# Two softmax attentions inside one kernel: turns placed ahead of the slabs' quarters, values' and outputs' low parts in other slots, quarters dealt with pauses

## Chip, cores and metric

The kernel runs on one core of one Trainium2 chip, as one launch. The metric is the time of the device in microseconds; the engines are PE (TensorE, matmuls and transposes), DVE (VectorE), ACT (ScalarE), POOL (GpSimd, which here issues the weight DMAs and negates weights) and SP (issues a few DMAs).

## What is computed

The reference is two transformer blocks, 512 tokens by 1024 channels, in float32. The change lies in two of its attentions, both over 16 heads of 64 channels:

```python
# first block: dilated windows; one mask and one bias by distance for all three groups
s = q @ k.T - slope * dist          # 512 x 512 per head, causal
p = exp(s - max); o = (p @ v) / sum(p)
x = x + (g_a * y_a + (g_b * (o @ w_attn_out))) @ w_out     # g = sigmoid(x @ w_gate)
# second block: attention over chosen keys
p = softmax(where(chosen, q @ k.T / 8, -inf)); o = p @ v
y = (o * silu(x @ w_g)) @ w_out_a
```

The kernel computes the first block's three dilated groups as one softmax over all keys with a bias for how many groups hold a key. Every matmul is three: each float32 operand is split into a high part (rounded for TensorE) and a low part, and high x high, low x high and high x low are added in PSUM.

## The kernel before

A stream of 231 weight slabs (128 x 1024 values, 512 KB) runs through four slots; POOL issues the two DMAs of each. A slab is 24 matmuls of 512 columns for one output tile of 128 channels. Between large projections stand the attentions, here called the first (`a`, over the phase "gates", 12 slabs) and the second (`b`, over the phase "g2", 8 slabs). Each attention walks over `PAIRS` = 8 pairs of heads. The order on each engine is the order in which the code is written, in three functions: `softmax_attention` for PE and one `attention` each for ACT and DVE. Semaphores tie them.

For pair i and query block q (0 to 3, the causal width is q+1 blocks):

- `scores(i, q)` on PE writes both heads' scores into one of two sets of banks (parity of q); `biased(i, q)` on DVE adds the bias or mask, takes the row extreme and stores to `PROBS`; `prob(i, q, h)` on ACT takes the exponential.
- `turn_p(i, q)` on PE transposes the probabilities into two "turn" banks; `pt_hi` (ACT) and `pt_lo` (DVE) copy the high and low parts to `PT_HI`, `PT_LO`, and only then is the bank free. `turn_p(i, 2)` needs the banks that `turn_p(i, 0)` and `turn_p(i, 1)` filled, `turn_p(i, 3)` those of `turn_p(i, 2)`, `turn_qk(i+2)` those of `turn_p(i, 3)`.
- `inverse` (DVE) and `spread` (ACT) make the inverse sums; `turn_inverse` (PE) transposes them into the out bank, from which `inverse_t` (ACT, first attention) or `inverse_gate` (DVE, second, times the gate) takes them to `INVERSE`.
- `values(i)` on PE needs `pt_lo(i, 3)`, `v_lo(i)` and `INVERSE`; `output(i)` on DVE takes its result, `out_hi` (ACT) and `out_lo` (DVE) split it.
- `turn_qk(i)`, `qk_hi(i)`, `qk_lo(i)` transpose and split the queries and keys of a pair, into the same two turn banks.

A slab of the weight phase is cut into quarters of 6 matmuls, which `fill(i, q)` deals out in four slots of a pair. `A_FILL` and `B_FILL` say how many quarters each slot gets, a row for each pair and one for the end. All slabs of an attention share one PSUM bank (`SLAB_BANK`), so a slab's first quarter waits until the slab before has been read: by a tanh on ACT (`gate`), in the second attention by a DVE instruction after it that reads the bank too. In the second attention two slabs are done ahead of the loop (`B_EARLY`), the second in the out bank.

Of the kernel before, what the change touches and what calls it, by code (L numbers as in the profile page):

```python
# [97 lines left out]
A_FILL = 5 * [[2, 1, 1, 2]] + 2 * [[1, 1, 1, 1]] + [[1, 1, 0, 0]] + [[4, 4]]  # L98
B_FILL = 6 * [[1, 1, 1, 0]] + [[1, 1, 1, 0]] + [[0, 0, 0, 0]] + [[2, 1]]
# [52 lines left out]
def program(nc, x, wstream, consts, small, lnv, out):  # L152
    with ExitStack() as ctx:
# [257 lines left out]
        def _(pe):  # L411
# [91 lines left out]
            def softmax_attention(a, name, table, early):  # L503
# [83 lines left out]
                for i in range(PAIRS):  # L587
                    scores(i, 0)
                    fill(i, 0)
                    if i:  # L590
                        turn_p(i - 1, 2)
                    scores(i, 1)
                    fill(i, 1)
                    if i:
                        turn_p(i - 1, 3)
                        turn_inverse(i - 1)
                    scores(i, 2)
# [6 lines left out]
                    fill(i, 3)  # L604
                    turn_p(i, 0)
                    turn_p(i, 1)
                turn_p(PAIRS - 1, 2)
# [213 lines left out]
        def _(act):  # L821
# [35 lines left out]
            def attention(a, sq, sk, name, table, early):  # L857
# [73 lines left out]
                for buf in (V_HI, V_LO):  # L931
                    for h in range(2):
                        d = slice((1 - h) * HD, (2 - h) * HD)
                        act.activation(buf[:, :, h, d], zero[:, 0:1].unsqueeze(2).to_broadcast([P, TT, HD]), ACT.Copy)\
                            .then_inc(sem(f"{a}_v_zero"), 1)
                qk_hi(0)
                for i in range(PAIRS):
                    last = i == PAIRS - 1
                    prob(i, 0, 0)
                    prob(i, 0, 1)  # L940
                    if i == 0 and early:
                        gate(0)
                    gates(i, 0)
                    if i:
                        pt_hi(i - 1, 2, 0)
                        pt_hi(i - 1, 2, 1)
                        spread(i - 1)
                    prob(i, 1, 0)
                    prob(i, 1, 1)
                    if i == 0 and early:  # L950
                        gate(1)
                    gates(i, 1)
                    if i:
                        pt_hi(i - 1, 3, 0)
                        pt_hi(i - 1, 3, 1)
                        if a == "a":
                            inverse_t(i - 1)
                    prob(i, 2, 0)
                    prob(i, 2, 1)
                    gates(i, 2)  # L960
                    if not last:
                        qk_hi(i + 1)
                    prob(i, 3, 0)
                    prob(i, 3, 1)
                    gates(i, 3)
                    pt_hi(i, 0)
                    pt_hi(i, 1)
                    v_hi(i)
                    if i:
                        out_hi(i - 1)  # L970
                i = PAIRS - 1
# [240 lines left out]
        def _(dve):  # L1212
# [32 lines left out]
            def attention(a, sq, sk, bias, name, table, early):  # L1245
                t0 = TILE0[name]

                def head_bias(i):
                    for h in range(2):
# [85 lines left out]
                if a == "a":  # L1335
                    head_bias(0)
                qk_lo(0)
                for i in range(PAIRS):
# [7 lines left out]
                    if i == 0 and early:  # L1346
                        gate(0)
                    gates(i, 0)
                    biased(i, 1)
                    if i:  # L1350
# [516 lines left out]
```

## Time and profile before

| | before |
|---|---|
| time, median of 3 runs | 1773.61 us (1773.6 to 1778.68) |
| the profiled execution's own time | 1777.48 us |
| its span, first to last instruction | 1775.4 us |
| mean granted clock of TensorE | 0.968 |
| PE busy | 1647.2 us (93%) |
| weight loads (PEld) | 1344.9 us (76%) |
| DVE, ACT, POOL busy | 928.3, 542.6, 589.6 us |
| first attention, 320.02 to 491.06 us | 171.04 us |
| second attention, 1164.87 to 1335.74 us | 170.87 us |

A "granted clock" of 1 is 2.4 GHz, of 0.5 is 1.2 GHz, and a number between is a stretch with both. Busy times of PE overlap from one matmul to the next, so the step from one start to the next start is what a matmul costs. The two attentions are named by the start of their first `scores` and the end of their last `values`.

### The profile page before, as it was taken

The page shows a single profiled execution, that of the slowest core. Times are in us where ns is not written, and L with a number is a line of the kernel's source. Part 1 is how long each engine was busy: PE and PEld are TensorE (multiplying, and loading weights), DVE is VectorE, ACT ScalarE, POOL GpSimd, SP SyncE. Part 2 cuts the span into 40 slices and gives each one's busy share as a digit, 9 for nine tenths or more (in the row PEclk, how much of TensorE's full clock was granted, in tenths as well). Part 3 has the DMA queues.
Part 4 walks back from the last instruction along what each step waited for, and adds up shares of the span by engine and source line. Part 5 has one row for each costly group of instructions (what it writes and reads, how often), then busy time and mean ns, then how long its engine had stood idle before and what let it go on. Part 6 is the DMA issues. An engine that isn't in the chain of part 4 may idle for free.

```text
span 1775.4 us, 20032 instructions
## 1 busy us (share of the span) xinstructions
PE 1647.2 (93%) x7808; PEld 1344.9 (76%) x7808; DVE 928.3 (52%) x1672; ACT 542.6 (31%) x1079; POOL 589.6 (33%) x698
## 2 busy tenths in 40 slices
PE   6999999999899899999998989978879799999985
PEld 5888878777787788888887768756658678888874
DVE  2999996466451444333001249835641606766654
ACT  3101131556400322222000130145540226667640
POOL 3445434221144344444443424411003232222211
PEclk9999999999999999999999999989989899999988
DMA  8888878443279698888886858832118484545434
GB/s 223 194 189 194 196 156 188 102 85 74 57 169 223 148 194 194 198 191 192 188 189 143 191 105 179 191 81 48 27 34 176 109 178 95 110 97 103 95 93 109
DMA packets 69134, 253.23 MB, mean 143 GB/s; under 512 B 7600, under 2 KB 7728, under 8 KB 68912
## 3 DMA queue, kind: packets, MB, share of 16 engines
q0 software_dynamic: 66528, 242.25, 63.3%
q1 hardware_dynamic: 1968, 7.60, 1.2%
q10 hardware_dynamic: 544, 2.10, 0.3%
q8 instruction: 62, 1.02, 0.2%
q14 instruction: 32, 0.26, 0.1%
HBM read 249.82 MB, written 2.10 MB: 142 GB/s over the span
## 4 chain that ended last, share of the span: by engine, by line
PE 85%; DVE 6%; ACT 5%; issue 2%; DMA 1%; SPq 0%; DVEq 0%; POOL 0%; ACTq 0%
PE PSUM L416 26%; PE PSUM L417 25%; PE PSUM L418 25%; PE PSUM L650 2%; ACT PROBS L878 2%; DVE PT_LO L1295 1%; PE PSUM L531 1%; PE PSUM L426 1%; ACT PT_HI L891 1%; PE PSUM L633 1%; PE PSUM L552 1%; PE PSUM L519 1%; DMA SMALLS<-small 1%; DVE MASK L1614 1%; DMA W_LO<-wstream 1%
## 5 line engine op out<-in xcount | busy, mean ns | idle before, releaser
L404 POOL DMA_DIRECT2D W_HI<-wstream x231 | 128.2, 555 | 1031.8 <-PE PSUM L418 1031.3
L416 PE MATMUL PSUM<-X_HI,W_HI 128*128 128x512 f32 x872 | 355.3, 407 | 29.4 <-DVEq L1312 17.6
L417 PE MATMUL PSUM<-X_LO,W_HI 128*128 128x512 f32 x872 | 345.6, 396 | 0.0
L418 PE MATMUL PSUM<-X_HI,W_LO 128*128 128x512 f32 x872 | 345.4, 396 | 0.0
L394 POOL TENSOR_SCALAR W_LO<-W_HI 128x1024 fp32r<-128x1024 f32 x231 | 253.2, 1096 | 20.4 <-DMA W_HI<-wstream 16.2
L416 PE MATMUL PSUM<-W_HI,X_HI 128*128 128x512 f32 x608 | 238.6, 392 | 9.2 <-DVE X_LO L1217 2.6
L398 POOL DMA_DIRECT2D W_LO<-wstream x231 | 208.3, 902 | 99.8 <-POOL W_LO L394 99.8
L417 PE MATMUL PSUM<-W_LO,X_HI 128*128 128x512 f32 x608 | 237.8, 391 | 0.0
L418 PE MATMUL PSUM<-W_HI,X_LO 128*128 128x512 f32 x608 | 237.8, 391 | 0.0
L416 PEld LDWEIGHTS PSUM<-X_HI,W_HI 128*128 128x128 f32 x872 | 166.7, 191 | 78.9 <-issue 43.7
L418 PEld LDWEIGHTS PSUM<-X_HI,W_LO 128*128 128x128 f32 x872 | 166.8, 191 | 36.6
L417 PEld LDWEIGHTS PSUM<-X_LO,W_HI 128*128 128x128 f32 x872 | 167.2, 192 | 32.4
L1475 DVE SCALAR_TENSOR_TENSOR CONV<-CONV_IN,SMALLS,CONV 128x512 f32<-128x512 f32 x240 | 186.3, 852 | 0.0
L416 PEld LDWEIGHTS PSUM<-W_HI,X_HI 128*128 128x128 f32 x608 | 115.0, 189 | 35.9 <-ACT INDEX_RELU L1107 3.1
L1562 DVE SCALAR_TENSOR_TENSOR GATE_A<-PSUM,SMALLS,GATE_A 128x511 f32<-128x511 f32 x88 | 66.0, 750 | 143.0 <-ACT GATE_A L1071 141.4
L418 PEld LDWEIGHTS PSUM<-W_HI,X_LO 128*128 128x128 f32 x608 | 114.8, 189 | 24.2
L417 PEld LDWEIGHTS PSUM<-W_LO,X_HI 128*128 128x128 f32 x608 | 114.9, 189 | 23.6
L878 ACT ACTIVATE PROBS<-PROBS,soft_stats 128x128 f32<-128x128 f32 (+3 forms) x128 | 70.9, 555 | 133.3 <-DVE soft_stats L1283 133.3
L855 ACT ACTIVATE QKV<-PSUM 128x512 f32<-128x512 f32 x48 | 24.8, 605 | 225.1 <-PE PSUM L418 225.1
L1243 DVE TENSOR_TENSOR GATE_B<-PSUM,GATE_B 128x512 f32<-128x512 f32 x16 | 9.9, 683 | 156.8 <-PE PSUM L418 156.8
L1295 DVE TENSOR_TENSOR PT_LO<-PSUM,PT_HI 128x256 fp32r<-128x256 f32 (+2 forms) x96 | 54.8, 598 | 70.9 <-ACT PT_HI L891 70.1
L1071 ACT ACTIVATE GATE_A<-PSUM,SMALLS 128x512 f32<-128x512 f32 x44 | 34.4, 782 | 165.9 <-PE PSUM L418 165.2
(226 smaller groups left out, 2668.7 us busy)
## 6 DMA issues: line engine op xcount, KB each, us to landing
W_HI<-wstream POOLq DMA_DIRECT2D x231, 512.0 KB, 4.0
W_LO<-wstream POOLq DMA_DIRECT2D x231, 512.0 KB, 5.9
GATE_A<-x SPq DMA_DIRECT2D x4, 512.0 KB, 6.1
GATE_B<-x SPq DMA_DIRECT2D x1, 2048.0 KB, 17.4
NORM_GAINS<-lnv ACTq DMA_DIRECT2D x2, 1024.0 KB, 5.5
out<-GATE_B SPq DMA_DIRECT2D x4, 512.0 KB, 2.8
CONST<-consts SPq DMA_DIRECT2D x1, 1032.0 KB, 10.9
SMALLS<-small SPq DMA_DIRECT2D x1, 245.0 KB, 12.1
```

The source lines that it names most:

```text
L394: pool.tensor_scalar(W_LO[:, r, :], W_HI[:, r, :].bitcast(F32), -1.0, 0.0, ALU.mult, ALU.add)\
L398: pool.dma_start(W_LO[:, r, :], wstream[n], accum_op=ALU.add).then_inc(w_lo_in[r], 16)
L404: pool.dma_start(W_HI[:, n % SLOTS, :], wstream[n]).then_inc(w_hi_in[n % SLOTS], 16)
L416: pe.matmul(o, lh, rh, start=start, stop=False)
L417: pe.matmul(o, lh, rl, start=False, stop=False)
L418: return pe.matmul(o, ll, rh, start=False, stop=stop)
L650: pe.matmul(o, m, part[:, h, w], start=False, stop=False, skip_group_check=True)
L878: act.activation(p, p, ACT.Exp, scale=-1.0, bias=soft_stats[:, 0, q, h:h + 1], accum_out=soft_stats[:, 1, q, h:h + 1]).then_inc(sem(f"{a}_ ...
L1071: act.activation(FFN_CONV[:, 2 * m + v, :], PSUM[:, 2 * m + v, :], ACT.Identity, scale=SMALLS[:, bass.ds(i * 12 + (S_AT["fw"].start + (2 * ...
L1295: dve.tensor_tensor(pt_block(PT_LO, both, q), src, pt_block(PT_HI, both, q).bitcast(F32), ALU.subtract).then_inc(sem(f"{a}_pt_lo"), 1)
L1475: dve.scalar_tensor_tensor(acc, src, w, acc, ALU.mult, ALU.add).then_inc(step, 1)
L1562: ins = dve.scalar_tensor_tensor(FFN_CONV[:, b, d:], PSUM[:, b, 0:SEQ - d], w, FFN_CONV[:, b, d:], ALU.mult, ALU.add)
```

## The change

Nothing is computed differently; the same instructions run in another order (a wait of DVE on its own earlier work is added in `head_bias`). On PE the turns of probabilities (and of the inverse) stand ahead of the slot's quarters where they stood behind. On ACT `pt_hi` is written ahead of `prob`, `v_hi(i-1)` moves from the end of pair i-1 to the second slot of pair i; in the second attention the two early gates go ahead of and behind `qk_hi(0)`. On DVE `v_lo(i-1)` and `out_lo(i-2)` move into pair i. The two tables of quarters are dealt anew, with an empty slot behind the end of most slabs.

```diff
-A_FILL = 5 * [[2, 1, 1, 2]] + 2 * [[1, 1, 1, 1]] + [[1, 1, 0, 0]] + [[4, 4]]
-B_FILL = 6 * [[1, 1, 1, 0]] + [[1, 1, 1, 0]] + [[0, 0, 0, 0]] + [[2, 1]]
+A_FILL = 2 * [[2, 2, 0, 2], [2, 0, 2, 2], [0, 2, 2, 0]] + [[2, 2, 0, 2], [2, 0, 0, 0]] + [[4, 4]]
+B_FILL = [[1, 1, 1, 1], [0, 1, 1, 1], [1, 0, 1, 1], [1, 1, 0, 1], [1, 1, 1, 0], [1, 1, 1, 1], [0, 0, 1, 0], [0, 1, 0, 0]] + [[2, 0]]
...
                     scores(i, 0)
-                    fill(i, 0)
                     if i:
                         turn_p(i - 1, 2)
+                    fill(i, 0)
                     scores(i, 1)
-                    fill(i, 1)
                     if i:
                         turn_p(i - 1, 3)
                         turn_inverse(i - 1)
+                    fill(i, 1)
                     scores(i, 2)
                     fill(i, 2)
...
                     scores(i, 3)
-                    fill(i, 3)
                     turn_p(i, 0)
                     turn_p(i, 1)
+                    fill(i, 3)
...
+                if early:
+                    gate(0)
                 qk_hi(0)
+                if early:
+                    gate(1)
                 for i in range(PAIRS):
                     last = i == PAIRS - 1
-                    prob(i, 0, 0)
-                    prob(i, 0, 1)
-                    if i == 0 and early:
-                        gate(0)
-                    gates(i, 0)
                     if i:
                         pt_hi(i - 1, 2, 0)
                         pt_hi(i - 1, 2, 1)
+                    prob(i, 0, 0)
+                    prob(i, 0, 1)
+                    gates(i, 0)
+                    if i:
+                        v_hi(i - 1)
                         spread(i - 1)
-                    prob(i, 1, 0)
-                    prob(i, 1, 1)
-                    if i == 0 and early:
-                        gate(1)
-                    gates(i, 1)
-                    if i:
                         pt_hi(i - 1, 3, 0)
                         pt_hi(i - 1, 3, 1)
                         if a == "a":
                             inverse_t(i - 1)
+                    prob(i, 1, 0)
+                    prob(i, 1, 1)
+                    gates(i, 1)
                     prob(i, 2, 0)
                     prob(i, 2, 1)
                     gates(i, 2)
                     if not last:
                         qk_hi(i + 1)
+                    pt_hi(i, 0)
+                    pt_hi(i, 1)
                     prob(i, 3, 0)
                     prob(i, 3, 1)
                     gates(i, 3)
-                    pt_hi(i, 0)
-                    pt_hi(i, 1)
-                    v_hi(i)
                     if i:
                         out_hi(i - 1)
+                v_hi(PAIRS - 1)
...
                 def head_bias(i):
+
+                    after(dve, "a_biased", 8 * i)
...
                     biased(i, 1)
                     if i:
+                        v_lo(i - 1)
                         pt_lo(i - 1, 3, 0)
                         pt_lo(i - 1, 3, 1)
-                    if i == 0 and early:
-                        gate(1)
+                        if a == "b":
+                            inverse_gate(i - 1)
                     gates(i, 1)
-                    if i and a == "b":
-                        inverse_gate(i - 1)
                     biased(i, 2)
+                    if i > 1:
+                        out_lo(i - 2)
...
                     gates(i, 3)
-                    v_lo(i)
-                    if i:
-                        out_lo(i - 1)
                     if a == "a" and not last:
                         head_bias(i + 1)
+                v_lo(PAIRS - 1)
+                out_lo(PAIRS - 2)
```

**PE, second attention, second pair (i = 1), around `scores(1, 1)`** (`[waits tile_free]` on a slab's first matmul is the wait for the shared slab bank). Before:

```order
L531 MATMUL PSUM<-QK_HI 128x256 [waits b_biased]
L531 MATMUL PSUM<-QK_HI 128x256
L531 MATMUL PSUM<-QK_LO,QK_HI 128x256 x2
L531 MATMUL PSUM<-QK_HI,QK_LO 128x256 x2
L416 MATMUL PSUM<-X_HI,W_HI 128x512 [waits tile_free,w_lo_in2]
L417 MATMUL PSUM<-X_LO,W_HI 128x512
L418 MATMUL PSUM<-X_HI,W_LO 128x512
L416 MATMUL PSUM<-X_HI,W_HI 128x512
L417 MATMUL PSUM<-X_LO,W_HI 128x512
L418 MATMUL PSUM<-X_HI,W_LO 128x512
L552 MATMUL PSUM<-CONST,PROBS 128x128 [waits b_pt_lo,b_exp]
L552 MATMUL PSUM<-CONST,PROBS 128x128 x3
```

After:

```order
L531 MATMUL PSUM<-QK_LO,QK_HI 128x256 x2
L531 MATMUL PSUM<-QK_HI,QK_LO 128x256 x2
L552 MATMUL PSUM<-CONST,PROBS 128x128 [waits b_pt_lo,b_exp]
L552 MATMUL PSUM<-CONST,PROBS 128x128 x3
L552 MATMUL PSUM<-CONST,PROBS 128x128 [waits b_pt_lo]
L552 MATMUL PSUM<-CONST,PROBS 128x128 x3
L562 MATMUL PSUM<-CONST,INVERSE 128x128 [waits tile_free,b_spread]
L562 MATMUL PSUM<-CONST,INVERSE 128x128 x3
L416 MATMUL PSUM<-X_HI,W_HI 128x512 [waits tile_free,w_lo_in2]
L417 MATMUL PSUM<-X_LO,W_HI 128x512
L418 MATMUL PSUM<-X_HI,W_LO 128x512
L416 MATMUL PSUM<-X_HI,W_HI 128x512
```

Before, the first quarter of a new slab (with `tile_free`) stood directly behind the scores and ahead of the turns of `PROBS`; now the turns of `PROBS` and of `INVERSE` stand ahead of it.

**ACT, second attention, end of pair 1 and start of pair 2** (`PT_HI` 128x2x128 and 128x2x2x128 are `pt_hi(1, 0)` and `pt_hi(1, 1)`, 128x3x128 is `pt_hi(1, 2)`). Before:

```order
L878 ACTIVATE PROBS,soft_stats<-PROBS,soft_stats 128x512 [waits b_biased] x2
L891 ACTIVATE PT_HI<-PSUM 128x2x128 [waits b_pv,b_pturned]
L891 ACTIVATE PT_HI<-PSUM 128x2x2x128 [waits b_pv,b_pturned]
L872 ACTIVATE V_HI<-QKV 128x4x64 [waits b_pv]
L872 ACTIVATE V_HI<-QKV 128x4x64
L908 ACTIVATE O_HI<-QKV 128x4x128 [waits b_o]
L878 ACTIVATE PROBS,soft_stats<-PROBS,soft_stats 128x128 [waits b_biased] x2
L891 ACTIVATE PT_HI<-PSUM 128x3x128 [waits b_pv,b_pturned] x2
L897 ACTIVATE INVERSE<-soft_stats 128x512 [waits b_o,b_inv]
L878 ACTIVATE PROBS,soft_stats<-PROBS,soft_stats 128x256 [waits b_biased] x2
```

After:

```order
L891 ACTIVATE PT_HI<-PSUM 128x2x128 [waits b_pv,b_pturned]
L891 ACTIVATE PT_HI<-PSUM 128x2x2x128 [waits b_pv,b_pturned]
L878 ACTIVATE PROBS,soft_stats<-PROBS,soft_stats 128x512 [waits b_biased] x2
L908 ACTIVATE O_HI<-QKV 128x4x128 [waits b_o]
L891 ACTIVATE PT_HI<-PSUM 128x3x128 [waits b_pv,b_pturned] x2
L878 ACTIVATE PROBS,soft_stats<-PROBS,soft_stats 128x128 [waits b_biased] x2
L924 ACTIVATE GATE_TANH<-PSUM 128x512 [waits b_gated,slab_done]
L872 ACTIVATE V_HI<-QKV 128x4x64 [waits b_pv]
L872 ACTIVATE V_HI<-QKV 128x4x64
L897 ACTIVATE INVERSE<-soft_stats 128x512 [waits b_o,b_inv]
L891 ACTIVATE PT_HI<-PSUM 128x4x128 [waits b_pv,b_pturned] x2
```

`pt_hi` now stands ahead of the exponentials of its slot, and `V_HI` stands between the narrow exponentials and the spread of `INVERSE` instead of ahead of `O_HI`.

**DVE, first attention, first pair (i = 0): `biased(0, 2)`, `qk_lo(1)`, the gate of slab 0 and `biased(0, 3)`** (ISA is `biased`; 128x384 is q = 2, 128x512 is q = 3). Before:

```order
L1283 ISA PROBS,soft_stats<-PSUM,HEAD_BIAS 128x384 [waits a_scores]
L1283 ISA soft_stats 128x1
L1283 ISA PROBS,soft_stats<-PSUM,HEAD_BIAS 128x384
L1283 ISA soft_stats 128x1
L1256 SCALAR_TENSOR_TENSOR QK_LO<-PSUM,qscale,QK_HI 128x512 [waits a_qk_hi]
L1256 SCALAR_TENSOR_TENSOR QK_LO<-PSUM,SMALLS,QK_HI 128x512 [waits a_qk_hi]
L1305 SCALAR_TENSOR_TENSOR GATE_A<-GATE_TANH,GATE_A 128x512 [waits tile_free]
L1283 ISA PROBS,soft_stats<-PSUM,HEAD_BIAS 128x512 [waits a_scores]
```

After:

```order
L1308 SCALAR_TENSOR_TENSOR GATE_A<-GATE_TANH,GATE_A 128x512 [waits tile_free]
L1286 ISA PROBS,soft_stats<-PSUM,HEAD_BIAS 128x384 [waits a_scores]
L1286 ISA soft_stats 128x1
L1286 ISA PROBS,soft_stats<-PSUM,HEAD_BIAS 128x384
L1286 ISA soft_stats 128x1
L1259 SCALAR_TENSOR_TENSOR QK_LO<-PSUM,qscale,QK_HI 128x512 [waits a_qk_hi]
L1259 SCALAR_TENSOR_TENSOR QK_LO<-PSUM,SMALLS,QK_HI 128x512 [waits a_qk_hi]
L1286 ISA PROBS,soft_stats<-PSUM,HEAD_BIAS 128x512 [waits a_scores]
```

The gate of slab 0, which needs the whole slab, now stands ahead of `biased(0, 2)` and so ahead of `qk_lo(1)`; before it stood behind both.

## Rows read from the trace of the kernel before

**Rows 1.** Busy time by stage: the second attention, then the first; columns as its head.

```profile
core 0: us, PE busy (x) PEld busy (x) DVE busy (x) ACT busy (x) POOL busy (x), PEclk, DMA share, GB/s
1164.87:1335.74 170.87, 137.47 (x777) 107.82 (x778) 90.55 (x244) 82.95 (x230) 15.86 (x19) 0.88 0.21 42
320.02:491.06 171.04, 157.44 (x921) 127.14 (x922) 93.88 (x250) 91.11 (x242) 30.16 (x36) 0.97 0.36 75
```

**Rows 2.** Waits of PE in the second attention: total, times, longest.

```profile
PE PSUM L416 <- DVEq L1312: 17.6, 5, 5.1
PE PSUM L552 <- DVE PT_LO L1295: 11.7, 13, 2.4
```

**Rows 3.** Timelines of ACT, DVE, PE: start us, us, instruction, [idle before <-releaser].

```profile
1185.59 0.57 ACT L924 ACTIVATE GATE_TANH<-PSUM 128x512 f32<-128x512 f32 x1
...
1187.51 0.68 DVE L1309 SCALAR_TENSOR_TENSOR GATE_A<-GATE_TANH,PSUM 128x512 f32<-128x512 f32 x1
...
1188.39 0.76 PE L416 MATMUL PSUM<-X_HI,W_HI 128*128 128x512 f32 x1 [4.56 <-DVEq L1312]
```

**Rows 4.** Windows after two long waits of PE, columns as in rows 1.

```profile
1188.00:1193.00 5.00, 4.61 (x16) 3.96 (x16) 1.16 (x6) 1.69 (x5) 0.00 (x0) 0.50 0.22 43
...
1292.00:1296.00 4.00, 4.00 (x28) 3.65 (x27) 1.61 (x4) 2.16 (x6) 0.00 (x0) 1.00 0.06 11
```

**Rows 5.** Waits of PE in the first attention.

```profile
PE PSUM L552 <- DVE PT_LO L1295: 8.6, 6, 2.4
PE PSUM L416 <- ACT GATE_B L915: 2.6, 3, 1.2
```

**Rows 6.** Timeline of PE at full clock, second attention, 1239 to 1257 us.

```profile
1239.48 0.87 PE L552 MATMUL PSUM<-CONST,PROBS 128*128 128x128 f32 x6
1240.29 0.33 PE L531 MATMUL PSUM<-QK_HI 64*128 64x128 f32 x2
...
1240.77 0.50 PE L416 MATMUL PSUM<-X_HI,W_HI 128*128 128x512 f32 x1
...
1246.89 1.06 PE L552 MATMUL PSUM<-CONST,PROBS 128*128 128x128 f32 x8 [0.83 <-DVE PT_LO L1295]
1247.79 0.60 PE L562 MATMUL PSUM<-CONST,INVERSE 128*128 128x128 f32 x4
...
1249.04 0.50 PE L416 MATMUL PSUM<-X_HI,W_HI 128*128 128x512 f32 x1
...
1250.53 1.04 PE L519 MATMUL PSUM<-CONST,QKV 128*128 128x128 f32 x8
1251.33 0.47 PE L416 MATMUL PSUM<-PT_HI,V_HI 128*128 128x512 f32 x1
...
1256.19 0.87 PE L552 MATMUL PSUM<-CONST,PROBS 128*128 128x128 f32 x6
```

**Rows 7.** Timeline of ACT at the same place.

```profile
1240.32 0.72 ACT L878 ACTIVATE PROBS<-PROBS,soft_stats 128x512 f32<-128x512 f32 x1 [2.64 <-DVE soft_stats L1283]
...
1242.49 0.71 ACT L872 ACTIVATE V_HI<-QKV 128x256 fp32r<-128x256 f32 x2
...
1244.90 0.40 ACT L878 ACTIVATE PROBS<-PROBS,soft_stats 128x128 f32<-128x128 f32 x1 [1.17 <-DVE soft_stats L1283]
...
1245.69 0.84 ACT L891 ACTIVATE PT_HI<-PSUM 128x384 fp32r<-128x384 f32 x2
1246.43 0.62 ACT L897 ACTIVATE INVERSE<-soft_stats 128x512 f32<-128x512 f32 x1
```

**Rows 8.** Timeline of DVE at the same place.

```profile
1242.15 1.17 DVE L1295 TENSOR_TENSOR PT_LO<-PSUM,PT_HI 128x256 fp32r<-128x256 f32 x2 [0.65 <-ACT PT_HI L891]
1243.24 0.75 DVE L1266 TENSOR_TENSOR V_LO<-QKV,V_HI 128x256 fp32r<-128x256 f32 x2
```

**Rows 9.** Chain of waits, first attention, pair 0: start us, us, what.

```profile
330.45 0.58 ACT QK_HI L865
331.05 1.41 DVE QK_LO L1256 x2
```

More of the change, by code:

```diff
@@ L1336, in attention @@
                     head_bias(0)
+                if early:
+                    gate(0)
                 qk_lo(0)
+                if early:
+                    gate(1)
                 for i in range(PAIRS):
@@ L1345, in attention @@
                         pt_lo(i - 1, 2, 1)
-                    if i == 0 and early:
-                        gate(0)
                     gates(i, 0)
@@ L1350, in attention @@
                     if i:
+                        v_lo(i - 1)
                         pt_lo(i - 1, 3, 0)
                         pt_lo(i - 1, 3, 1)
-                    if i == 0 and early:
-                        gate(1)
+                        if a == "b":
+                            inverse_gate(i - 1)
                     gates(i, 1)
-                    if i and a == "b":
-                        inverse_gate(i - 1)
                     biased(i, 2)
+                    if i > 1:
+                        out_lo(i - 2)
                     if not last:
```

## Prediction

> **What bounds the kernel now.** I read the busy time by stage first. Both attentions take 171 us. In the first PE is busy 157.4 of 171.0 us at a granted clock of 0.97; in the second 137.5 of 170.9 us at 0.88 [rows 1]. DVE and ACT are busy 83 to 94 us in each, about half. So no engine but PE is near its limit, and what can be won are PE's waits and the half clock (1.2 GHz) that follows some of them. The rest of the kernel is untouched and comes into the sum at nothing: the weights that the attentions use are far ahead (POOL has 15.9 us of work in 171), and the phases around them keep their order.
>
> Next the waits of PE. In the second attention two groups make 29.3 of its 33.4 idle us: 17.6 us in 5 waits on the gate's DVE instruction, the longest 5.1 us, and 11.7 us in 13 waits of the turns of `PROBS` on `PT_LO` [rows 2]. In the first, 8.6 us are turns on `PT_LO`, 2.6 us are waits on the gate's tanh [rows 5]; its gate releases the bank from ACT alone, so this wait is short there.
>
> Last the single rows. The 4.56 us wait at 1188.39 shows the chain of a bank's release: ACT's tanh starts at 1185.59, the DVE instruction only at 1187.51 behind other work, and PE's quarter follows 0.2 us after its end [rows 3]. The quarter then runs at half clock: the window behind it has a granted clock of 0.50 [rows 4].
>
> **What a pair costs PE.** From start to start at full clock [rows 6]: `turn_p(0)` and `(1)` 0.81 (1239.48 to 1240.29), `scores(0)` 0.48, `turn_p(2)` again six transposes, 0.81, `scores(1)` 0.55 (between `scores(0)` and the next one), `turn_p(3)` 0.90, `turn_inverse` and `scores(2)` 1.25, `turn_qk` 0.80, `values` and `scores(3)` 4.86: 10.46 us. A quarter is 1.49. The second attention is 8 x 10.46, less 0.8 for the first `turn_qk` that lies ahead of it, plus 24 quarters: 82.9 + 35.8 = 118.7 us. Its stretch is 170.9, so 52.2 us are lost: 33.4 idle [rows 1], and some 19 by half clock and by stops inside groups.
>
> **The new order, walked once.** Let T be the end of `scores(i, 3)`; in the rows T is 1239.5.
> ACT: before, the wide exponentials began at T+0.8 and `pt_hi` stood behind them; DVE was free at T+2.0 but waited 0.65 us for it and began `pt_lo(i, 0)` at T+2.7 [rows 7, 8]. Now `pt_hi(i, 0)` and `(i, 1)` run until T+1.5, so `pt_lo` begins at T+2.0 and, at 1.17 us for the two [rows 8], ends at T+3.1. The exponentials (0.72 each) then end at T+2.9, `out_hi` at T+3.5, `pt_hi(i, 2)` (0.74 from start to start) at T+4.3, the narrow exponentials (0.79) at T+5.1, `v_hi` (0.71) at T+5.8, `spread` (0.62) at T+6.4 [rows 7].
> PE, with a quarter in both slots: 0.81 + 1.49 + 0.48 brings `turn_p(i, 2)` to T+2.8; its first half needs `pt_lo(i, 0)` (T+2.4), its second `pt_lo(i, 1)` (T+3.1): no wait. Then 0.81 + 1.49 + 0.55 + 0.90 bring `turn_inverse` to T+6.5, against `spread` at T+6.4: no wait, but no slack either. `values` comes at about T+11, long after `pt_lo(i, 3)` (T+8.3), `v_lo` and `inverse_gate` (T+8.9). So `v_lo` (0.75 [rows 8]) and `out_lo` cost nothing where they now stand; DVE covers them in PE's `values`, and `biased(i+1, 0)` comes over 1 us earlier.
>
> **An empty slot** behind `scores(i, 3)` leaves PE at `turn_p(i, 2)` until T+3.5 in any case: 1.5 us of waiting in the quarter's place. One behind `turn_p(i, 2)` is the same, 1.5 us, at `turn_inverse`. A gate on ACT in the chain adds 0.57 [rows 3]. Empty slots behind `turn_inverse` and `scores(2)` cost nothing. In return no quarter meets an unread bank: the shortest pause is two turns and two scores plus a chain that is over by then. The bank waits, 17.6 us, go.
>
> **Second attention, stalls that I count.** Pair 0: 0.4 on `qk_lo(1)`. Turns of pair 0 with slot (1, 0) empty: 1.5. Gate at (2, 0): 0.55. Slot (4, 3): 1.5. (6, 0), behind a gate: 2.0. (6, 3) and (7, 0): 3.0. End: `turn_p(7, 2)` 1.95, `values(7)` behind the last gate, `pt_lo` and `inverse_gate` 1.85. Sum 12.8, say 13 us. Half clock: the 18.8 us that are lost beside the idle time, over some ten waits of 1.9 us or more in this stretch, are 1.9 us for each; most of these waits go, and I keep 5 us, for the start and two of the waits in the last pairs. 118.7 + 13 + 5 = 136.7 us against 170.9: **34.2 us** less.
>
> **First attention, by differences.** Gone: 2.6 us of bank waits [rows 5] and 0.3 us of a smaller one, about 1 us because more quarters come in twos without a new start, and 2 us of half clock in the last pair, whose waits shrink. The turns' waits: today all of PE's idle time is 13.6 us [rows 1]. New: pair 0 waits 2.5 us, since the gate of slab 0 now stands ahead of `biased(0, 2)`, and `qk_hi` 0.58 a piece and `qk_lo` 1.41 [rows 9] come after it, with nothing between `scores(0, 3)` and the turns that need their bank. Slots (2, 0) and (5, 0) are empty with a gate and `head_bias` on DVE ahead of `pt_lo(i, 2)`: 2.5 us each. (2, 3) and (5, 3): 1.5 each. Gates at (1, 0), (4, 0), (7, 0): 0.4 each. Pair 7: 0.95 and 1.95. Sum 14.7, so 1.1 more than today. Net: 2 + 1 - 1.1, **1.8 us** less.
>
> **Sum.** 36 us off the profiled execution's 1777.5 gives 1741.5. The median of the runs lies 3.9 below it, so 1773.6 - 36 = 1737.6, rounded 1738. Changes under 0.3% (5 us) can't be told from none.
>
> **A rule that speaks against it.** The window behind the 4.56 us wait was at 0.50, but the one behind a 2.64 us wait at 1290, with transposes and `values` in it, stayed at 1.00 [rows 4]; so what decides is not the wait's length alone. The Trainium skill (TensorE: Matmul & The Clock Gate, Part 4: PE-mode transpose) says that transposes do not count as busy for the clock gate as matmuls do. The second of these windows does not show it. What it would do is the second rival.
>
> **Rivals.**
> - *The clock stays low.* Turns now stand together (fourteen to eighteen transposes with scores, no quarter between) beside waits of 1.5 to 2.5 us, at 12 places: 7 in the second attention, 5 in the first. At about 2 us of half clock each, 24 us, against some 7 counted, the time is 17 us higher, 1755. For it: the half clock after waits in [rows 4]; against: the second window there. By the rule of the Trainium skill named above this is the number.
> - *Everything fits.* The empty slots cost only half of what I walked, because engines start a little ahead of my sums, and no half clock is left: 13 + 5 us less 6 and 5, 1727, and down to 1722 if the first attention's three 2.5 us waits fall too.
> - *The waits only move.* The slabs' quarters no longer wait for a bank, but the turns, now ahead of them, wait for `PT_LO` as long: 17.6 us of one kind become 17 of another. Then 1773. Against: the chain of `pt_hi` and `pt_lo` is shortened by 0.7 us in each pair, and the bank waits hung on DVE's late gate, not on it.
> - *Slower: `spread` is late.* `turn_inverse` has no slack against the chain exponentials, gate, `v_hi`, `spread`. PE passes it 14 times. The change loses from where the chain is 36/14 = 2.6 us longer per pair than walked; at 3.2 us it is 1782. ACT would have to take half again as long as its rows say (6.4 us); it is busy only 83 us of 171 [rows 1].
>
> **Chances and range.** Forecast, 1730 to 1746: 0.63. Low clock, 1746 to 1765: 0.17. Everything fits, under 1730: 0.13. Waits only move: 0.04. Slower: 0.03. Faster by over 0.3% is 0.93, within it 0.04, slower 0.03. The range 1726 to 1754 takes the forecast, over half of the low clock and a third of the third case, 0.8 in all.
>
> **What would show it.** Right: the second attention near 137 us, PE's waits on the gate gone, waits on `PT_LO` or `INVERSE` under 2 us and only at the empty slots, granted clock 0.95 or more there; the first attention 167 to 171 us, with a wait of some 2 us before the first turns of `PROBS`. Wrong: steady waits of `turn_inverse` on `spread` in every pair (the chain on ACT mis-sized), a clock still under 0.9 in the second attention, or a first attention that is over 3 us longer than before.

## Result and profile after the change

| | before | after |
|---|---|---|
| time, median of 5 runs each in the same comparison | 1777.84 us | 1746.81 us |
| ratio, 95% interval | | 0.983 (0.9811 to 0.9849) |
| first attention | 171.04 us | 178.57 us; 177.04 to 179.32 in three other executions |
| second attention | 170.87 us | 132.22 us; 130.61 to 134.39 in six other executions |

The change takes 31 us off. The forecast was 1738 us with a range of 1726 to 1754, so the time lies 9 us above the number and within the range. The forecast counted 36 us off 1773.61, the median of the first three runs of before; the five runs have 1777.84, so 4.2 of the 9 us are this shift and 5 are a gain that is smaller than forecast. The two attentions do not share the gain as forecast: against the one trace of before the second gives 36.5 to 40.3 us back (forecast 34.2), and the first, which should have won 1.8 us, loses 6.0 to 8.3.

The profiled execution after the change took 1828.19 us, and those of e1 to e4, e10 and e11 below 1821 to 1876, since PE waited 72 to 98 us for the DMA of weights ahead of the first attention, where it waited for none before; the attentions come after these waits. Rows below are from that execution after the change unless said otherwise. Another profiled execution of the same kernel (the run e12 below) had a time of 1748.8 us, and there the account closes: first attention 8.3 us more, second 36.5 less, everything else 0.5 less, 28.7 us against the 1777.5 of before.

Windows over the two attentions, the answer to [rows 1]; columns as there. First the profiled execution after the change, then the other execution of the same kernel.

```profile
400.50:579.07 178.57, 161.81 (x921) 130.31 (x922) 100.31 (x250) 92.45 (x242) 30.21 (x36) 0.94 0.34 71
1254.59:1386.81 132.22, 121.18 (x777) 96.19 (x778) 87.08 (x243) 82.23 (x228) 15.99 (x19) 0.99 0.26 55
```

```profile
319.10:498.42 179.32, 163.00 (x921) 131.56 (x922) 100.43 (x250) 92.56 (x242) 30.16 (x36) 0.92 0.34 71
1172.99:1307.38 134.39, 123.85 (x777) 98.78 (x778) 87.11 (x243) 82.37 (x228) 15.97 (x19) 0.96 0.26 55
```

In the second attention PE's idle time went from 33.4 to 11.0 us, and its busy time, the same 777 matmuls, from 137.5 to 121.2: the clock was 0.99 where it was 0.88. In the first, PE is both idler (16.8 us, before 13.6) and slower (161.8 us for the same 921 matmuls, before 157.4; clock 0.94, before 0.97).

Waits of PE in the second attention, the answer to [rows 2]: total, times, longest.

```profile
PE PSUM L552 <- DVE PT_LO L1298: 7.3, 6, 1.6
PE PSUM L416 <- DVE INVERSE L1324: 2.2, 1, 2.2
PE PSUM L531 <- DVE QK_LO L1259: 1.6, 1, 1.6
PE PSUM L562 <- ACT INVERSE L897: 1.2, 4, 0.5
```

The group on the gate's DVE instruction, 17.6 us before, is gone, and the turns' 11.7 us in 13 waits are 7.3 in 6. In the first attention, the answer to [rows 5]:

```profile
PE PSUM L552 <- DVE PT_LO L1298: 10.2, 5, 3.1
PE PSUM L552 <- DVE QK_LO L1259: 3.5, 2, 3.2
```

Here the turns wait for `PT_LO` fewer times but longer, and a new wait of 3.2 us on `QK_LO` has come in pair 0. The three long ones, in a timeline of PE (start, us, instruction, idle before and releaser):

```profile
416.01 0.41 PE L552 MATMUL PSUM<-CONST,PROBS 128*128 128x128 f32 x2 [3.22 <-DVE QK_LO L1259]
...
445.97 1.06 PE L552 MATMUL PSUM<-CONST,PROBS 128*128 128x128 f32 x8 [3.15 <-DVE PT_LO L1298]
...
506.83 1.94 PE L552 MATMUL PSUM<-CONST,PROBS 128*128 128x128 f32 x8 [3.14 <-DVE PT_LO L1298]
```

They are pair 0 and the empty slots (2, 0) and (5, 0); slot (i, q) is the place of `fill(i, q)`, and it is empty where the table has 0. Behind each the granted clock is down to its lower level for some us. Windows of the execution of 1748.8 us at the same three waits, which end at 333.5, 364.4 and 426.0 us (the windows begin up to 2 us before):

```profile
332.00:339.00 7.00, 5.51 (x16) 4.31 (x17) 5.09 (x11) 3.51 (x8) 0.00 (x0) 0.55 0.40 71
364.00:369.00 5.00, 4.58 (x17) 4.23 (x18) 3.48 (x10) 4.31 (x14) 0.00 (x0) 0.50 0.51 88
424.00:430.00 6.00, 4.00 (x16) 3.74 (x17) 5.05 (x17) 4.29 (x13) 0.34 (x1) 0.57 0.66 124
```

### The profile page after: what moved, and what is told of

Read it like the earlier page. It is cut to its first block, busy times and chain, and to the rows that moved or that the text cites. A ratio compares the mean times of both kernels' runs of the same rounds, so it can differ in the third digit from the quotient of the medians.

```text
span 1826.1 us, 20032 instructions
## 1 busy us (share of the span) xinstructions
PE 1643.9 (90%) x7808; PEld 1340.8 (73%) x7808; DVE 919.2 (50%) x1672; ACT 543.6 (30%) x1079; POOL 668.1 (37%) x698
## 4 chain that ended last, share of the span: by engine, by line
PE 83%; POOL 5%; DVE 4%; ACT 3%; DMA 2%; issue 2%; SPq 0%; DVEq 0%; ACTq 0%
PE PSUM L416 25%; PE PSUM L417 24%; PE PSUM L418 24%; POOL W_LO L394 5%; PE PSUM L650 2%; PE PSUM L531 2%; DMA W_LO<-wstream 1%; PE PSUM L552 1%; PE PSUM L426 1%; PE PSUM L633 1%; DVE MASK L1619 1%; PE PSUM L519 1%; DMA SMALLS<-small 1%; PE PSUM L635 1%; PE PSUM L634 1%
## 5 line engine op out<-in xcount | busy, mean ns | idle before, releaser
L404 POOL DMA_DIRECT2D W_HI<-wstream x231 | 130.6, 565 | 995.4 <-PE PSUM L418 994.9
L394 POOL TENSOR_SCALAR W_LO<-W_HI 128x1024 fp32r<-128x1024 f32 x231 | 332.4, 1439 | 30.1 <-DMA W_HI<-wstream 26.0
L416 PE MATMUL PSUM<-W_HI,X_HI 128*128 128x512 f32 x608 | 243.6, 401 | 81.4 <-DMA W_LO<-wstream 74.5
L417 PE MATMUL PSUM<-W_LO,X_HI 128*128 128x512 f32 x608 | 241.7, 397 | 0.0
L1480 DVE SCALAR_TENSOR_TENSOR CONV<-CONV_IN,SMALLS,CONV 128x512 f32<-128x512 f32 x240 | 173.9, 800 | 0.0
L878 ACT ACTIVATE PROBS<-PROBS,soft_stats 128x128 f32<-128x128 f32 (+3 forms) x128 | 70.8, 558 | 41.7 <-DVE soft_stats L1286 41.5
L416 PE MATMUL PSUM<-W_HI,FFN_HI 128*128 128x512 f32 x176 | 69.5, 395 | 0.0
## 6 DMA issues: line engine op xcount, KB each, us to landing
GATE_B<-x SPq DMA_DIRECT2D x1, 2048.0 KB, 16.8
```

The lines of the kernel that those rows point to most:

```text
L394: pool.tensor_scalar(W_LO[:, r, :], W_HI[:, r, :].bitcast(F32), -1.0, 0.0, ALU.mult, ALU.add)\
L404: pool.dma_start(W_HI[:, n % SLOTS, :], wstream[n]).then_inc(w_hi_in[n % SLOTS], 16)
L416: pe.matmul(o, lh, rh, start=start, stop=False)
L417: pe.matmul(o, lh, rl, start=False, stop=False)
L878: act.activation(p, p, ACT.Exp, scale=-1.0, bias=soft_stats[:, 0, q, h:h + 1], accum_out=soft_stats[:, 1, q, h:h + 1]).then_inc(sem(f"{a}_ ...
L1480: dve.scalar_tensor_tensor(acc, src, w, acc, ALU.mult, ALU.add).then_inc(step, 1)
```

## Experiments

All numbers of a stretch are from one profiled execution of each kernel, from the start of the first `scores` to the end of the last `values`. Stretches are what is compared. The whole times and ratios that the expectations of e1 to e4 name stay untested: e2 to e4 took 1813 to 1891 us and e1 1747 to 1850, beside 1776 to 1881 for the kernel before. The wait added in `head_bias` stays in every run but that of the kernel before.

Stretches repeat without a change in their code, and so show how far one execution lies from the next:

| stretch, order and table | us |
|---|---|
| first attention, before (before, e2, e10) | 171.04, 169.46, 169.44 |
| first attention, changed (after, e1, e3, e12) | 178.57, 177.16, 177.04, 179.32 |
| second attention, before (before, e3) | 170.87, 172.11 |
| second attention, changed (after, e1, e2, e4, e7, e11, e12) | 132.22, 130.61, 130.71, 130.65, 133.64, 133.85, 134.39 |

So a difference under 2.5 us in the first attention, or under 4 in the second, is read only with the waits behind it.

**The change again.**

> The changed kernel itself, for a second profile. Theory: as in its first profile, the second attention takes 132 us (38.7 less than before) and the first 178.5 us (7.5 more), and the whole is 31 us faster than before. Rival: the 7.5 us in the first attention belong to that one execution, whose weights came late in its first 320 us; then the first attention takes 167 to 171 us here, as forecast.

Measured: 177.16 us and 130.61 us. The first attention's loss and the second's gain repeat.

**One attention at a time.** The code keeps both orders and chooses by the attention's name; each attention takes the order and table of before or of the change.

```diff
+NEW = 'b'                      # e2; 'a' in e3
-                turn_qk(0)
-                for i in range(PAIRS):
-                    scores(i, 0)
...
+                if a in NEW:   # order of the change
+                    turn_qk(0)
...
+                else:          # order of before
+                    turn_qk(0)
```

> New order and new table in the second attention alone, the first as before. Theory (the two attentions add up): 38 to 39 us faster than before, ratio 0.978, and so 7 us faster than the whole change. Rival (the first attention's change is neutral and the second gives only 31 us): the same time as the whole change, ratio 0.983.

Measured: first attention 169.46 us, second 130.71.

> New order and new table in the first attention alone, the second as before. Theory: 7 to 8 us slower than before, ratio 1.004. Rival: the same time within 2 us, ratio 1.000.

Measured: first 177.04 us, second 172.11, with the waits of before in it to the tenth (17.6 us in 5 on the gate, 11.7 in 13 on `PT_LO`). So the two attentions add up, and nothing beyond the spread passes from one to the other: the second gains what it gains by its own edits, and so the first loses.

**The new order with the table of before in the first attention.**

```diff
-A_FILL = 2 * [[2, 2, 0, 2], [2, 0, 2, 2], [0, 2, 2, 0]] + [[2, 2, 0, 2], [2, 0, 0, 0]] + [[4, 4]]
+A_FILL = 5 * [[2, 1, 1, 2]] + 2 * [[1, 1, 1, 1]] + [[1, 1, 0, 0]] + [[4, 4]]
```

> The whole change, but the first attention keeps its old table of quarters (two quarters at the end and at the start of a pair, one in each middle slot) with the new order. Theory (the first attention loses by the table: empty slots behind a gate, and slab 0 done by slot 1): its stretch falls to 160 to 165 us, the whole to 44 to 49 us faster than before, ratio 0.973 to 0.975. Rival (it loses by the new order on ACT and DVE, head_bias and gate ahead of the low parts): its stretch stays at 171 us or above and the whole is at best 39 us faster, ratio 0.978.

Measured: first attention 160.26 us, second 130.65. The new order by itself takes 9 to 11 us off the first attention (169.44 to 171.04 before), and the new table gives 17 to 19 us back.

**A second table for the second attention,** with e4's first attention. It fills the slots behind `scores(3)` and puts the empty ones behind `turn_inverse` and `scores(2)`.

```diff
-B_FILL = [[1, 1, 1, 1], [0, 1, 1, 1], [1, 0, 1, 1], [1, 1, 0, 1], [1, 1, 1, 0], [1, 1, 1, 1], [0, 0, 1, 0], [0, 1, 0, 0]] + [[2, 0]]
+B_FILL = [[1, 1, 0, 1], [1, 1, 1, 1], [1, 1, 1, 1], [1, 1, 0, 1], [1, 0, 1, 1], [1, 0, 0, 1], [1, 0, 0, 1], [1, 0, 0, 1]] + [[1, 0]]
```

> The new order in both attentions; the first with the table of before, the second with a table that fills every slot behind scores(i, 3) and every slot behind turn_p(i, 2) but (0,2)'s neighbours, and puts its empty slots behind turn_inverse and scores(i, 2), where they are held to cost nothing. Theory (only the empty slots behind scores(3) and turn_p(2) cost): in e4 the second attention took 130.65 us with 7.3 us of waits on PT_LO and 2.2 on INVERSE; (1,0), (2,0), (4,3), (6,0), (6,3) and (7,0) made some 6 of these. All of them filled: second attention 123 to 126 us, first as in e4 160 to 161. Beside the kernel before 171.06 + 170.87 - 160.3 - 124.5 = 57 us less. Rival (an empty slot costs PE the same wherever it stands, since the chain on ACT and DVE is the bound of the pair): second attention stays at 129 to 132 us, the waits stand then at turns of PROBS in other pairs.

Measured: first attention 160.71 us, second 127.45; median of 5 runs 1723.32 us against 1778.93 for the kernel before, ratio 0.9688 (0.9675 to 0.9702). This is the fastest version found, 23 us under the change's median. The second attention missed its 123 to 126 by 1.5 us. Its waits of PE:

```profile
PE PSUM L417 <- DVE INVERSE L1396: 3.2, 2, 2.0
PE PSUM L532 <- DVE QK_LO L1331: 1.6, 1, 1.6
PE PSUM L553 <- DVE QK_LO L1331: 1.6, 2, 1.4
PE PSUM L553 <- DVE PT_LO L1370: 1.1, 2, 0.9
PE PSUM L563 <- ACT INVERSE L921: 1.0, 4, 0.2
```

The waits for `PT_LO` of the turns of `PROBS` fell from 7.3 to 1.1 us, with 0.5 us more at one `turn_qk`: an empty slot costs by its place, as the theory has it. But the empty slot (0, 2) laid bare 1.4 us of `qk_lo(1)` in pair 0, and `values(6)` now waits for `inverse_gate(6)` too (1.2 us); I had not priced either.

**The new order with both old tables.**

> The new order in both attentions, both tables as before. Theory (in the second attention the order takes the bank waits away and the table is worth a little): the old table leaves slot 3 of every pair empty, at 1.1 to 1.5 us each, 8 to 12 us, and the last pair without quarters; second attention 133 to 140 us, no waits on the gate's DVE instruction in slots 1 and 2 beyond 0.5 us. First attention 160 to 161. Rival (the pauses of the new table take the bank waits away): the waits of PE on the gate stay near 17 us and the second attention is over 150 us.

Measured: first 160.73 us, second 139.69. The waits on the gate were 1.7 us in 2, both in slot 2 and 0.84 us long where none over 0.5 was expected, the turns' on `PT_LO` 9.4 in 9, of which six are 1.14 us each at the old table's empty slots behind `scores(3)`.

**The old order with both new tables.**

> The order of before in both attentions, with both tables of the change. With e6 (new order, old tables: 160.7 and 139.7 us) and the changed kernel (178 and 132) it makes the four corners. Theory (order and table are two things: the order takes away the bank waits, the pauses by themselves take away few of them, since the gate's DVE instruction stands late whatever the table): second attention 158 to 170 us against 170.9, waits of PE on the gate still over 8 us; first attention 178 to 186, since its empty slots cost there too. Rival (the pauses do most of it): second attention 140 to 150 us.

Measured: first 180.29 us, second 154.01; time 1771.29 us. Neither statement held for the second attention: it was 17 us shorter without any new order. Its waits of PE:

```profile
PE PSUM L553 <- DVE PT_LO L1370: 16.2, 12, 3.2
PE PSUM L417 <- DVE INVERSE L1396: 5.3, 3, 2.2
PE PSUM L417 <- DVEq L1387: 2.7, 1, 2.7
```

The pauses alone cut the bank waits from 17.6 to 2.7 us, and the turns, still behind the quarters, wait longer (16.2 for 11.7). With e6 and the changed kernel this makes four corners, in us:

| order, table | first attention | second attention | waits on the gate in the second |
|---|---|---|---|
| old, old (before, e2, e3, e10) | 169.4 to 171.0 | 170.9 to 172.1 | 17.6 |
| old, new (e9) | 180.3 | 154.0 | 2.7 |
| new, old (e6; e4 and e5 for the first) | 160.3 to 160.7 | 139.7 | 1.7 |
| new, new (the change) | 177.0 to 179.3 | 130.6 to 134.4 | none |

In the second attention the order by itself is worth 31 to 32 us and the table 17 to 18, and together they are worth 36.5 to 41.5, less than the sum, since either alone takes nearly all of the bank waits. In the first the order is worth 9 to 11, and the table costs 9 to 11 with the old order and 16 to 19 with the new.

**One row of the first attention's table.**

```diff
-A_FILL = 2 * [[2, 2, 0, 2], [2, 0, 2, 2], [0, 2, 2, 0]] + ...
+A_FILL = [[2, 1, 1, 2], [2, 0, 2, 2], [0, 2, 2, 0]] + [[2, 2, 0, 2], [2, 0, 2, 2], [0, 2, 2, 0]] + ...
```

> The changed kernel with one row of the first attention's table as before: pair 0 has [2, 1, 1, 2] for [2, 2, 0, 2], so that slab 0 is full at slot (0,2) and its gate no longer stands ahead of biased(0, 2). Theory (the 3.2 us wait in pair 0, with the half clock behind it, comes of the gate of slab 0 ahead of the biases and exponentials that the turns of PROBS wait for): first attention 172 to 174.5 us for 177.2, the wait in pair 0 under 1.5 us, granted clock of the stretch 0.95. Rival (the wait hangs on the start of the chain alone, qk_hi and qk_lo of pair 1): first attention 176 to 178, the wait in pair 0 still near 3 us. Second attention as in e1, 130 to 132.

Measured: first attention 175.66 us, second 133.64. The wait in pair 0 fell from 3.22 to 0.70 us and the clock no longer fell behind it. The stretch missed the expected 172 to 174.5 and lies outside the rival's 176 to 178 too: it was 1.4 to 3.7 us shorter than the four with the table of the change, where the theory asked for 2.7 to 5.2. The wait itself is accounted for, the half clock behind it is within the spread. And the gate was less than half of the cause. In e12 `scores(0, 2)` ends at 328.35 us, DVE takes it up at 330.09 behind the gate, and the turn starts at 333.49: 5.14 us. In e7 the same three are 327.86, 327.90 and 331.89: 4.03 us, 1.1 less, though ACT's tanh now stands ahead of `qk_hi(1)`. The other 1.4 of the 2.5 us are the quarter that now stands behind `scores(0, 2)`, where PE works while the chain runs.

**Two quarters one slot earlier.**

```diff
-A_FILL = 2 * [[2, 2, 0, 2], [2, 0, 2, 2], [0, 2, 2, 0]] + ...
+A_FILL = 2 * [[2, 2, 0, 2], [2, 0, 2, 2], [2, 0, 2, 0]] + ...
```

> The changed kernel with two rows of the first attention's table altered: pairs 2 and 5 have [2, 0, 2, 0] for [0, 2, 2, 0], the same quarters one slot earlier. Theory (an empty slot (i, 0) with a gate on ACT and DVE ahead of the chain costs 3.1 us of waiting and about 2 us of half clock, an empty slot (i, 1) nothing): 2 x 4 to 2 x 5 us less, first attention 168 to 170 for 177 to 178. Rival (the pause costs the same in slot 1, at turn_inverse or turn_qk): 175 to 178. Second attention 131 to 133.

Measured: first attention 169.40 us, second 133.85. The two waits of 3.15 us are 0.39 us, and the windows behind them are no longer slow (450.3 to 454.3 and 506.9 to 510.9 us, granted clock 1.00). The first attention is 7.6 to 9.9 us shorter, as the theory had it; the second lies 0.9 over what was expected. An empty slot (i, 0) behind a gate costs some 4.3 us, an empty slot (i, 1) nothing that shows. With e7 (2.4 us against the mean of the four) this explains some 11 of the table's 16 to 19 us. The rest would be the slots (2, 3) and (5, 3) with 1.14 us each, and pair 7, whose wait of 1.88 us also has half clock behind it; those were not tried apart.

**`V_HI` and the low parts of values and outputs back in their old slots,** in the kernel of e4.

```diff
                         gates(i, 3)
+                        v_hi(i)              # ACT
...
-                            v_hi(i - 1)
                             spread(i - 1)
...
-                            v_lo(i - 1)      # DVE
                             pt_lo(i - 1, 3, 0)
...
-                        if i > 1:
-                            out_lo(i - 2)
...
                         gates(i, 3)
+                        v_lo(i)
+                        if i:
+                            out_lo(i - 1)
```

> The kernel of e4 (new order in both, first attention with the table of before) with v_hi, v_lo and out_lo back in the slots that they had before: v_hi(i) on ACT behind gates(i, 3), v_lo(i) and out_lo(i - 1) on DVE behind gates(i, 3), ahead of biased(i + 1, 0). Theory of the prediction (biased(i+1, 0) comes over 1 us earlier by their going, and turn_inverse has no slack against spread): each pair is 0.7 to 1.5 us longer, each attention 5 to 12 us longer than in e4: first 165 to 172, second 136 to 143. Rival (the slots of the low parts do nothing; the turns ahead of the quarters and pt_hi ahead of the exponentials do it all): both within 1.5 us of e4, 160 and 131.

Measured: first attention 166.07 us, second 138.34: 5.8 and 7.7 more than e4. The rival is out: these slots are worth 10 to 13.5 us in the kernel of e4, with the spread of the second attention taken off for the lower end. How the gain is shared between ACT's `V_HI` and DVE's low parts was not tried. But they do not cost each pair the same. PE in the second attention, three of its ten waits for `PT_LO`:

```profile
1176.80 1.06 PE L553 MATMUL PSUM<-CONST,PROBS 128*128 128x128 f32 x8 [2.10 <-DVE PT_LO L1369]
...
1210.37 1.06 PE L553 MATMUL PSUM<-CONST,PROBS 128*128 128x128 f32 x8 [0.38 <-DVE PT_LO L1369]
...
1259.51 1.43 PE L553 MATMUL PSUM<-CONST,PROBS 128*128 128x128 f32 x8 [2.63 <-DVE PT_LO L1369]
```

A pair with quarters in its slots waits 0.38 us at `turn_p(3)`, where it waited nothing; the slots (1, 0) and (6, 0), empty, wait 2.10 and 2.63, before 1.43 and 1.50, and behind them the clock falls (PE busy in the stretch 123.7 us for 119.6).

**The early gates alone,** in the kernel before.

```diff
+                if early:
+                    gate(0)
                 qk_hi(0)             # likewise qk_lo(0) on DVE
+                if early:
+                    gate(1)
...
-                    if i == 0 and early:
-                        gate(0)
```

> The kernel before with one edit of the change: the gates of the second attention's two early slabs stand on ACT ahead of qk_hi(0) and behind it, and on DVE ahead of qk_lo(0) and behind it, no longer in pair 0. Theory: pair 0 of the second attention loses its waits for the bank, and the second attention is 5 to 6 us shorter, 165 to 166 us; the first stays at 171. Rival (the start is hidden behind qk_hi and qk_lo, on which PE waits anyway): second attention within 1.5 us of 170.9.

Measured: second attention 167.63 us, first 169.44. The waits on the gate went from 17.6 us in 5 to 14.9 in 4: one wait of 2.7 us is gone and nothing more. Neither the 5 to 6 us nor the rival's 1.5 was right, it is 3.2 us, or 4.5 against the second attention of e3. The first attention's 169.44 for the expected 171 comes without a change in its code, as in e2.

**The change a third time.**

> The changed kernel once more, for its stretches and the spread between executions: first attention 177 to 179 us, second 130.5 to 133.5, time 1744 to 1748.

Measured: 179.32 and 134.39 us, 0.3 and 0.9 over; the four runs took 1742.7 to 1774.1 us, median 1746.89, ratio 0.9809 (0.9789 to 0.9828).

## Why the prediction was right, and where it was not

**The number and its luck.** The time lies in the range, but errors of both signs made it up. In e12's profiled execution the first attention is 10.1 us over its forecast of 169.2, the second 2.3 us under its 136.7, and the rest 0.5 under; in other executions the second is up to 6.1 under. The shift of the median before, 4.2 us, was in no part of the forecast. The sign that the prediction named for being wrong, a first attention over 3 us longer, came.

**What bounds the kernel.** Right. PE runs the same matmuls in both stretches, and what was won or lost there are its waits and its half clock; outside the two stretches 0.5 us moved.

**The second attention, forecast 34.2 us less.** Right, a little low: idle time 11.0 us where I counted 13, and half clock 0 to 4 us where I counted 5 (the busy time is 119.6 us in e4 at a clock of 1.00, 123.9 at most). The bank waits went. A slot that is empty behind `scores(3)` costs 1.14 us for the 1.5 that I walked, (1, 0) and (6, 0) cost 1.6 and 1.7 with the 0.20 us of `turn_inverse` behind them (1.5 and 2.0 walked). My reason was too narrow in one point: I wrote that the bank waits go because the turns and scores stand between a slab's end and the next quarter. They do (e6), but the table's pauses would have done it without the order (e9).

**The walk of the pair.** `turn_inverse` was to come at T+6.5 against `spread` at T+6.4, without slack. It waits 0.20 us behind the empty slots (1, 0) and (6, 0), 0.25 us with a gate in the chain at (2, 0), where 0.55 was counted, 0.53 us in pair 7, and nowhere else, so the sum was right to 0.3 us. That `v_lo` and `out_lo` cost nothing where they now stand is right, and that they cost something where they stood is shown by e8, though at `turn_p(3)` and in the empty slots above all, not at `turn_inverse`.

**The first attention, forecast 1.8 us less, measured 6.0 to 8.3 more.** This holds the part of the miss that is the kernel's, and the step that failed is the half clock behind the new waits, which the forecast put at nothing. In the execution of 179.32 us the idle time is 16.3 us; I had 14.7 (the terms as written add up to 14.6). The busy time is 163.0, 5.6 more than before, and I had 3 less: 1 for quarters in twos, which no run measures by itself, and "2 us of half clock in the last pair, whose waits shrink". That term can stand against the trace of before: the clock is low there twice in the last pair, from 464 and from 474 us, and once in each execution after the change; but in e2 and e10, with the code of before, it is low only once as well. What is missing is the half clock behind pair 0 and the slots (2, 0) and (5, 0), which stands in each of the four profiled executions with this table. I took it at about 2 us a place for the rival, the clock that stays low, but none of it for the forecast.

**The clock that stays low.** In the first attention this rival came true at three places, and in the second hardly at all. The reason given there does not tell them apart. The sequence of `scores`, six transposes, `scores`, a wait, and twelve transposes stands at (2, 0) and (5, 0) of the first attention with a wait of 3.15 us, and at (1, 0) and (6, 0) of the second with 1.43 and 1.50. Behind the long waits, those of pair 0 included, the clock fell in 15 of 15 instances; behind the short ones in 2 of 14 (two in each of seven executions). In e11 the waits at (2, 0) and (5, 0) are 0.39 us and the clock did not fall, though there quarters stand between the transposes too. So the length of the wait fits the cases, and the transposes alone do not; no run changed the one without the other. The Trainium skill (TensorE: Matmul & The Clock Gate, Part 4: PE-mode transpose), which the prediction names, says that transposes do not count as busy for the clock gate as matmuls do. In e1, e2 and e4 the trace does not show an effect of that: the whole second attention ran at 1.00. The prediction's own argument that the length does not decide was weak, since of its two windows the one behind the longer wait was slow; the better row is the window 1214.5 to 1218.5 us of before, at 0.57 behind a wait of 2.65 us, beside the 1.00 behind 2.64.

**Why those waits were 3.15 us and not 2.5.** Slot (2, 0) on three engines, DVE first, then ACT, then POOL:

```profile
441.75 1.79 DVE L1308 SCALAR_TENSOR_TENSOR GATE_A<-GATE_TANH,GATE_A 128x512 f32<-128x512 f32 x1 [1.44 <-ACT GATE_TANH L919]
443.46 1.40 DVE L1253 SCALAR_TENSOR_TENSOR HEAD_BIAS<-CONST 128x512 f32<-128x512 f32 x2
...
445.27 1.01 DVE L1298 TENSOR_TENSOR PT_LO<-PSUM,PT_HI 128x384 fp32r<-128x384 f32 x2
```

```profile
441.03 0.69 ACT L919 ACTIVATE GATE_TANH<-PSUM,half_gate_b 128x512 f32<-128x512 f32 x1 [0.75 <-PE PSUM L418]
```

```profile
441.36 0.55 POOL L404 DMA_DIRECT2D W_HI<-wstream  x1 [12.39 <-PE PSUM L418]
441.93 1.06 POOL L394 TENSOR_SCALAR W_LO<-W_HI 128x1024 fp32r<-128x1024 f32 x1
```

The gate's DVE instruction took 1.79 us; in the trace of before seven of its eight instances take 0.68. The last matmul of a slab releases two things at once, ACT's tanh (and DVE's gate behind it) and POOL's preparation of the next weights. DVE's gate reads two operands in SBUF, and POOL's `W_LO` instruction (1.06 us) lies wholly within it. Nearly all gates of the first attention are like that, as the tile's instructions show (ns: least, median, most), before and after:

```profile
L1305 DVE SCALAR_TENSOR_TENSOR GATE_A<-GATE_TANH,GATE_A x8: 681/682/1782, 332.4 to 488.0; 128x512 f32<-128x512 f32 x8
```

```profile
L1308 DVE SCALAR_TENSOR_TENSOR GATE_A<-GATE_TANH,GATE_A x8: 678/1787/1790, 410.9 to 576.0; 128x512 f32<-128x512 f32 x8
```

Before, DVE came to seven of the eight gates late, behind other work, when POOL's `W_LO` instruction was over: 0.68 us. Since the change DVE stands waiting for the gate in seven of eight, starts at the same event as POOL, and takes 1.79. Without these 1.11 us the waits at (2, 0) and (5, 0) would be 2.04 us by this estimate, under the 2.5 that I walked, with no reason in the walk for 3.15. The Trainium skill (SBUF — State Buffer, Who interferes with whom) says that a DVE instruction with two SBUF inputs contends with a GpSimd instruction that reads SBUF, and that the ports they share are an exclusive lock. The trace agrees, 0.68 + 1.06 = 1.74 for 1.79; in e4, where the `W_LO` instruction starts 0.01 us after two of the gates for 0.17 us, these take 1.62. In the second attention the gate's DVE instruction reads PSUM and takes 0.69 us also where the `W_LO` instruction lies over it. The longer gate costs only where PE has nothing to do meanwhile: in e11 the gates at the same two places take 1.79 us too, and the waits are 0.39. I read this from the traces; no run moved POOL's work away.

**The other rivals.** That the waits only move is true in part for the order of before with the new tables (e9: 14.9 us fewer at the bank; 4.5 more on `PT_LO` at the turns of `PROBS`, 1.5 at `turn_qk`, and 2.6 more on `INVERSE`), and not for the change. `spread` was not late. "Everything fits", 1727 us, is about what e5 reached (1723), by other tables.

## What to carry to other kernels

A wait is not priced by its length alone: price each wait of some 3 us that a schedule makes with the half clock behind it (here 1 to 2 us more each: e11 took 2.8 us off each of two waits and 3.8 to 5.0 off the stretch for each), and fill its slot first. Cost an empty slot by what stands next in the queue: where the next operation needs the result of a chain that has just begun, it costs what of the chain nothing covers (1.1 to 3.2 us here), elsewhere little (nothing that shows at (2, 1) in e11, 1.2 us at (0, 2) in e5). And when a helper engine's instruction is moved so that it starts on the same event as another engine's, look up which operands both take from SBUF; its duration in the old trace may be one that it had only because it came late. Above all, when an edit has an order and a table, or two stages, forecast and try them apart: here one part gained 9 to 11 us in the same stretch in which another lost 16 to 19.

## What the runs showed of the hardware

The granted clock did not fall after the same wait each time. Behind the waits of 3.14 to 3.22 us it fell in every profiled execution, and behind the one of 1.88 us in pair 7 too (six of six). Behind a wait of 1.50 us in slot (6, 0) of the second attention, and behind one of 1.62 at its end, it stayed up in one execution of the changed kernel and fell in another, with the same instructions on both sides. First the one (behind each wait), then the other:

```profile
1349.60:1353.60 4.00, 3.79 (x25) 2.83 (x25) 3.94 (x13) 3.04 (x10) 0.00 (x0) 1.00 0.77 132
...
1376.00:1380.00 4.00, 4.00 (x24) 3.43 (x25) 2.45 (x7) 3.06 (x8) 0.39 (x1) 1.00 0.00 0
```

```profile
1268.00:1272.00 4.00, 4.00 (x17) 2.78 (x16) 3.44 (x8) 2.79 (x10) 0.00 (x0) 0.58 0.58 112
...
1294.50:1298.50 4.00, 4.00 (x14) 3.10 (x15) 2.73 (x7) 2.84 (x8) 0.00 (x0) 0.59 0.00 0
```

That is what the second attention differs by from one execution to the next. PE's idle time in it is 10.5 to 11.0 us in all seven; the stretch takes 130.6 to 130.7 us where the clock is never low in it (e1, e2, e4), 132.2 where it is low once (0.99), 133.6 and 133.9 where twice (e7, e11), and 134.4 where three times (0.96). Each time costs 0.5 to 1.6 us. And DVE's gate with both operands in SBUF took 0.68 us alone and 1.79 us with POOL's `W_LO` instruction over it.
